# A fused three-layer block on one core: value projection spread over the heads, gate projection split, embedding projections moved

## The chip, the cores and the metric

The kernel runs on one core of a Trainium2 chip. The metric is the device time of one execution in microseconds (us), lower is better. The engines are TensorE (PE, with its weight loads PEld), VectorE (DVE), ScalarE (ACT), GpSimd (POOL) and SyncE (SP), which issues the DMAs of the weights. Each has its own stream of instructions, in order, and they meet through semaphores.

## The reference, cut to what matters

256 tokens of width 1024 pass through one block (adaptive modulation, sparse attention and convolution, feed-forward net, two layer norms) and then through two layers of another kind:

```
def second_block(x, p, ...):
    for i in range(2):
        hn = rms_norm(h, norm_mix[i])
        mix = gla_mixer(hn, ...) if i == 0 else diff_attn_mixer(hn, ...)
        h = h + mix
        h = h + swiglu_2(rms_norm(h, norm_ffn[i]), ffn_w_in[i], ffn_w_out[i])
        gate = jax.nn.sigmoid(rms_norm(h, ple_norm[i]) @ ple_w_gate[i])
        h = h + gate * (p[i] @ ple_w_proj[i])

def gla_mixer(h, w_in, w_gate_f, b_gate_f, w_gate_b, b_gate_b, g_out, w_out):
    q, k, v, r, zf, zb = split_cols(h @ w_in, [512, 512, 1024, 1024, 16, 16])
    la_f = heads(log_sigmoid(zf @ w_gate_f + b_gate_f) / 16, 128)
    ...
def diff_attn_mixer(h, ...):
    q, k, v = split_cols(h @ w_in, [1024, 1024, 1024])     # q, k: normed and rotated
    ... 8 heads: softmax of two score maps, a = p0 - lam * p1, o = a @ v ...
```

## The kernel before

Activations lie transposed, as 8 tiles of 128 channels by 256 tokens. Weights come in slabs of 512 output columns. A slab is loaded into one of two buffers `raw`, in ring order. ScalarE rounds it into `whi` and VectorE writes the rest `raw - whi` into `wlo` (function `low`), each in four quarters. The activations are split the same way (`ohi`, `olo`, for the differential layer `dhi`, `xlo`), and a product is three matmuls (`three`): high by high, low by high, high by low. Each projection is a phase of `plan()`; `gemm` on each engine walks its slabs and tiles, and the slab that follows is split during the one before it. The order on each engine is written out by hand.

The places that the change touches:

- `layer_norm` closes each sublayer of the first block. TensorE sums values and squares over channels. VectorE and ScalarE make mean, variance and scale (`rstd`), centre and scale `res`, and write `ohi`, `om`, `olo` tile by tile. TensorE fills the wait with `keep_warm`.
- The gated layer begins with `gla_z` (48 rows, in float32, from `om`), then `gla_q`, the sums of squares (`stats`), another `keep_warm`, the two gate products from `g_z`, and `gla_k`, `gla_v`, `gla_r`. The squares are added on POOL.
- Before its four heads ScalarE computes both halves of `silu(r)` and then the first `kd_tok`, which TensorE waits for.
- `ple(k)`: the projection `ple_proj{k}` (48 matmuls, copied by ScalarE into `pp`), then `stats`, then `ple_gate{k}`, two slabs, whose tiles VectorE scales (`gt`), ScalarE puts through the sigmoid (`sg`), POOL multiplies by `pp` (`prod`) and VectorE adds to `res`. After the first of them VectorE and ScalarE also make the operand `dhi`, `xlo` of `diff_q` from each tile.
- The differential layer: `diff_q`, `diff_k`, `diff_v`, then 8 heads: TensorE scores, VectorE maximum (`neg_max`), ScalarE exponential (`d_p`), VectorE weights, TensorE transposes, ScalarE copy (`d_pt`), TensorE product with `d_v`, VectorE copy (`d_o`). Then `out2`.

A phase whose first slab is in `WIDE` takes the channel tiles in the outer loop, so all four output tiles go on as soon as one operand tile is there. SP frees a `raw` buffer by a table: `reader_done = {"split": lo_ready, ..., "pe": z_done}`; `gla_z` is of kind `pe`.

## Time and profile before

| | us |
|---|---|
| median of 3 runs (range) | 1118.05 (1114.88 to 1119.05) |
| the profiled execution | 1114.69 |
| its span in the profile | 1112.5 |
| TensorE busy, share of the span | 1055.4, 95% |
| VectorE busy | 724.4, 65% |
| ScalarE busy | 555.6, 50% |

The span is what the trace covers of the profiled execution; 2.2 us lie outside it. TensorE's busy time is modelled from pipelined matmuls, so the rate is better read from the start of one to the start of the next. The granted clock of TensorE is given as a share of 2.4 GHz; its two levels are 1.00 and 0.50.

### The profile page before, as it was taken

Reading aid. Unit: us, or ns where it says so; the run is one execution under the profiler, and the core shown is the slowest. Engines: PE = TensorE matmul, PEld = TensorE weight load, DVE = VectorE, ACT = ScalarE, POOL = GpSimd, SP = SyncE. Lnnn points to the kernel's source line nnn. Section 1 sums busy time; section 2 is a strip of 40 time slices with the busy share of each in tenths; the row PEclk is TensorE's granted clock in tenths of the full one; section 3 lists DMA queues with packets and bytes.
Section 4 is the critical chain, followed back from the end, with each engine's and each line's share of the span. In section 5 each row is a group of like instructions: output and inputs, shape, how many; then the busy total and the mean of one; then the engine's idle time right before and its main releaser. Section 6 shows DMA issues by size and latency. Waiting matters only on the chain. (4 is left out here: it accounts for less than half of the span.)

```text
span 1112.5 us, 20252 instructions
## 1 busy us (share of the span) xinstructions
PE 1055.4 (95%) x7893; PEld 979.4 (88%) x7893; DVE 724.4 (65%) x1130; ACT 555.6 (50%) x958; POOL 225.1 (20%) x246
## 2 busy tenths in 40 slices
PE   6899998999999899999999999979987999999998
PEld 5577787999999698889999999978865999999997
DVE  5788758777655567767565656676768765655654
ACT  2224466545454676337545444656447754544453
POOL 0000013333312121022333311131110223332101
PEclk9989899999999999999999999989999999999999
DMA  9984452577557354404646455644440266554651
GB/s 352 401 308 158 143 199 76 175 262 263 150 156 221 99 216 149 155 1 163 216 155 222 115 158 183 228 151 152 152 152 1 94 210 205 172 163 139 191 189 39
DMA packets 183587, 192.78 MB, mean 173 GB/s; under 512 B 5913, under 2 KB 143426, under 8 KB 183522
## 3 DMA queue, kind: packets, MB, share of 16 engines
q1 hardware_dynamic: 182512, 191.15, 50.8%
q8 instruction: 43, 0.70, 0.3%
q0 software_dynamic: 144, 0.52, 0.2%
q10 hardware_dynamic: 866, 0.21, 0.1%
q14 instruction: 22, 0.18, 0.0%
HBM read 190.83 MB, written 1.05 MB: 172 GB/s over the span
## 5 line engine op out<-in xcount | busy, mean ns | idle before, releaser
L1395 DVE TENSOR_TENSOR wlo<-raw,whi 128x1024 fp32r<-128x1024 f32 (+2 forms) x316 | 360.8, 1187 | 69.8 <-ACT whi L892 69.3
L2089 PE MATMUL gemm<-ohi,whi 128*128 128x256 f32 x1376 | 387.4, 282 | 3.6 <-DVE olo L1435 1.7
L2090 PE MATMUL gemm<-olo,whi 128*128 128x256 f32 x1376 | 384.5, 279 | 0.0
L2091 PE MATMUL gemm<-ohi,wlo 128*128 128x256 f32 x1376 | 383.3, 279 | 0.0
L892 ACT ACTIVATE whi<-raw 128x1024 fp32r<-128x1024 f32 (+2 forms) x316 | 280.6, 954 | 62.1 <-PE gemm L2091 49.4
L2089 PEld LDWEIGHTS gemm<-ohi,whi 128*128 128x128 f32 x1376 | 258.5, 188 | 7.0 <-issue 4.5
L2090 PEld LDWEIGHTS gemm<-olo,whi 128*128 128x128 f32 x1376 | 258.7, 188 | 0.6 <-issue 0.5
L2091 PEld LDWEIGHTS gemm<-ohi,wlo 128*128 128x128 f32 x1376 | 258.6, 188 | 0.0
L2091 PE MATMUL gemm<-acthi,wlo 128*128 128x256 f32 x528 | 147.7, 280 | 0.0
L2089 PE MATMUL gemm<-acthi,whi 128*128 128x256 f32 x528 | 147.7, 280 | 0.0
L2090 PE MATMUL gemm<-actlo,whi 128*128 128x256 f32 x528 | 147.3, 279 | 0.0
L727 POOL TENSOR_TENSOR prod<-sg,ut 128x256 f32<-128x256 f32 x66 | 51.4, 780 | 263.1 <-DVE ut L1796 160.9
L2091 PEld LDWEIGHTS gemm<-acthi,wlo 128*128 128x128 f32 x528 | 99.2, 188 | 0.0
L2090 PEld LDWEIGHTS gemm<-actlo,whi 128*128 128x128 f32 x528 | 99.1, 188 | 0.0
L2089 PEld LDWEIGHTS gemm<-acthi,whi 128*128 128x128 f32 x528 | 98.9, 187 | 0.0
L1172 ACT ACTIVATE sg<-gt 128x256 f32<-128x256 f32 x66 | 27.6, 419 | 131.5 <-DVE gt L1796 91.4
L731 POOL TENSOR_TENSOR actlo<-prod,acthi 128x256 f32 (+1 forms) x63 | 70.3, 1116 | 0.0
L2090 PE MATMUL gemm<-xlo,whi 128*128 128x256 f32 x224 | 63.9, 285 | 0.0
L1796 DVE TENSOR_TENSOR ut<-gemm,rstd 128x256 f32<-128x256 f32 x44 | 18.4, 419 | 52.1 <-PE gemm L2091 52.1
L764 POOL TENSOR_TENSOR sq_sum<-sq_sum,dsq 128x256 f32<-128x256 f32 x28 | 24.1, 862 | 110.3 <-ACT dsq L911 99.1
L2321 PE MATMUL gemm<-om,raw 128*128 128x256 f32 x192 | 45.6, 395 | 0.0
L2089 PE MATMUL gemm<-dhi,whi 128*128 128x256 f32 x128 | 40.0, 313 | 5.6 <-DVE xlo L1432 4.4
(367 smaller groups left out, 1535.9 us busy)
## 6 DMA issues: line engine op xcount, KB each, us to landing
raw<-in_ffn_w_in SPq DMA_DIRECT2D x44, 1024.0 KB, 6.2
raw<-in_ffn_w_out SPq DMA_DIRECT2D x32, 704.0 KB, 5.8
part<-in_w_ada SPq DMA_DIRECT2D x32, 512.0 KB, 10.3
raw<-in_gla_w_in SPq DMA_DIRECT2D x6, 2048.0 KB, 7.8
raw<-in_diff_w_in SPq DMA_DIRECT2D x6, 2048.0 KB, 7.7
raw<-in_w_gate SPq DMA_DIRECT2D x11, 1024.0 KB, 6.3
raw<-in_w_up SPq DMA_DIRECT2D x11, 1024.0 KB, 8.5
raw<-in_w_down SPq DMA_DIRECT2D x16, 704.0 KB, 5.4
```

What stands on the lines that cost most here:

```text
L727: pool.tensor_tensor(tl(prod, j), tl(sg, j), tl(ut, j), ALU.mult).then_inc(prod_done, 1)
L731: pool.tensor_tensor(tl(actlo, t - 1), tl(prod, 1 - j), tl(acthi, t - 1).bitcast(F32), ALU.subtract).then_inc(actlo_ready, 1)
L764: pool.tensor_tensor(sq_sum[:, :], sq_sum[:, :], src, ALU.add).then_inc(squares_summed if last else sq_added, 1)
L892: act.activation(whi[hslot][:, q * w:(q + 1) * w], src[:, q * w:(q + 1) * w], ACT.Copy).then_inc(hi_ready, 1)
L1172: act.activation(tl(sg, j), tl(gt, j), ACT.Silu).then_inc(silu_done, 1)
L1395: dve.tensor_tensor(wlo[hslot][:, q * w:(q + 1) * w], src[:, q * w:(q + 1) * w], whi[hslot][:, q * w:(q + 1) * w].bitcast(F32), ALU.subtra ...
L1796: ins = dve.tensor_tensor(dst, bank[:, 0:T], rstd[:, 0:T], ALU.mult)
L2089: pe.matmul(dst, st_hi, mv_hi, start=start, stop=False)
L2090: pe.matmul(dst, st_hi, mv_lo, start=False, stop=False)
L2091: return pe.matmul(dst, st_lo, mv_hi, start=False, stop=stop_)
L2321: ins = pe.matmul(G[t][:, 0:T], w[:, k, t * P:(t + 1) * P], tl(om, k), start=k == 0, stop=k == KT - 1)
```

## The change

Four groups of edits.

- **Layer norms**: ScalarE squares the mean straight from the sums in PSUM, VectorE makes the variance before the mean, centres the first two tiles singly, and makes `om` of tile 0 itself.
- **Start of the gated layer**: the first embedding projection takes the place of `keep_warm`. `gla_q` comes first and is `WIDE`; the eight squares are added on VectorE; `gla_z` comes behind `stats` and is split in three like the others. ScalarE's second half of `silu(r)` comes behind the first `kd_tok`.
- **Embedding projections**: the phases `ple_proj1` and `ple_proj2` are gone. Their weights have buffers of their own, are split in `down0` and `ple_gate1`, and their matmuls (`projection_of`) stand in the layer norm and between `ple_gate1` and `diff_q`. `ple(k)` begins with `ple_gate{k}`, with `stats` behind its first tile.
- **Values**: `diff_v` is cut into 64 steps of three matmuls with 256 columns. 16 stand before the heads and six in each head. The scores wait for their own pair of rotated tiles only. The splits of the second value slab and of `out2`'s first slab move into the heads.

In the order ScalarE's and SP's edits, then VectorE's, then TensorE's:

```diff
-    ple = lambda k: [Phase(f"ple_proj{k}", 1, 2048, 8, 1), Phase(f"ple_gate{k}", 2, SLAB, 4, 1)]
+    ple = lambda k: [Phase(f"ple_gate{k}", 2, SLAB, 4, 1)]
...
-        WIDE = ("gate_up0", "out1", "out2")
+        WIDE = ("gate_up0", "gla_q", "out1", "out2")
...
+            def load_projection(n):
+                sp.wait_ge(tile_done, (PH["gate_up0"].tile0 + 4, PH["down1"].tile0 + KT)[n])
+                sp.dma_start(flat(pw[n], 2, D), kmaj(a["ple_w_proj_2"][n], 0, D)).then_inc(pw_in, 16)
...
-                me.next(mean_ready)
-                me.did(act.activation(sq_sum[:, :], mean[:, :], ACT.Square), mean_squared)
+                me.next(mean_done)
+                me.seen(mean_done)
+                me.did(act.activation(sq_sum[:, :], X[0][:, 0:T], ACT.Square, scale=1.0 / D), mean_squared)
...
-            gemm("gla_q")
+            for q in range(3):
+                ahead(PH["gla_q"], At(0), q)
             root(X[0], T + 2, 1.0 / D, 1, rstd[:, :])
+            ahead(PH["gla_q"], At(0), 3)
...
-                gemm(f"ple_proj{k}", evac(lambda at, t: tl(pp, t), pp_ready))
                 root(X[0], T, 1.0 / D, 1, rstd[:, 0:T])
...
+                    if k == 1 and m in (1, 2):
+                        projection_split(1, m - 1)
...
+            take_projection(0, 1, 2)
             log_exp()
             next_quarters("diff_q")
             root(X[0], T + 2, 1.0 / D, 1, rstd[:, :])
+            take_projection(3)
...
+                if i in (2, 5, 7):
+                    take_values({2: 1, 5: 2, 7: 3}[i])
+                if 3 <= i <= 6:
+                    ahead(*OUT2, i - 3)
                 if i == 6:
                     pair_root(0, X[1])
...
-                center(0)
-                center(2)
+                center(0, 1)
+                center(1, 1)
                 me.next(sd_ready)
...
                 scale(0, 1)
+                me.again(normed)
+                me.link(dve.tensor_scalar(tl(om, 0), tl(res, 0), g[:, 0:1], b[:, 0:1], ALU.mult, ALU.add))
                 scale(1, 1)
+                rest_alone(0)
+                center(2)
+                me.again(centered)
                 scale(2, 2)
-                rest(0)
                 center(4)
                 rest(1)
...
+            for n, copies in pp_copies(1):
+                dve.wait_ge(pp_done, n + 1)
+                for dst, bank in copies:
+                    ins = dve.tensor_copy(dst, bank)
+                ins.then_inc(pp_ready[0], 1)
+            dve.wait_ge(z_hi_ready, 1)
+            dve.tensor_tensor(z_lo[:, :], raw[PH["gla_z"].slot][:, 0:384], z_hi[:, :].bitcast(F32),
+                              ALU.subtract).then_inc(z_lo_ready, 1)
+            for t in range(1, KT):
+                dve.wait_ge(sq_ready, SQUARED + t + 1)
+                me.link(dve.tensor_tensor(sq_sum[:, :], tl(sq, 0) if t == 1 else sq_sum[:, :], tl(sq, t), ALU.add),
+                        gla_summed if t == KT - 1 else None)
-            for q in range(4):
+            for q in range(3):
                 low(PH["gla_k"], At(0), q)
             root()
...
+                    if k == 1 and m in (2, 3):
+                        projection_low(1, m - 2)
...
+                if i in (0, 1):
+                    low(*VALUES, 2 + i)
+                if 4 <= i <= 7:
+                    low(*OUT2, i - 4)
...
-                gemm(f"ple_proj{k}", pp_ready, shape="ple")
-                stats()
-                gemm(f"ple_gate{k}", ple_in, olo_from=start)
+                def after(at, t):
+                    if (at.i, t) == (0, 0):
+                        stats()
+                gemm(f"ple_gate{k}", ple_in, olo_from=next_operand(), after=after)
...
             layer_norm()
-            keep_warm(X[2], 4)
+            projection_of(0)
...
-            gemm("diff_v", v_ready, shape="token", operand=(dhi, xlo), after=lambda at, t: partners(6 + t) if at.i == 0 else None)
-            pe.wait_ge(qk_ready, 8)
-            pe.wait_ge(v_ready, 8)
+            value_steps(0, 8)
+            partners(6)
+            partners(7)
+            value_steps(8, 16)
...
             for i in range(NH + 2):
                 if i + 1 < NH:
                     scores(i + 1)
+                if i >= 2:
+                    h = i - 2
+                    banks.claim(X[2], mixed_ready)
+                    me.next(pt_ready)
+                    if h % 2 == 0:
+                        pe.wait_ge(v_ready, 4 + h // 2 + 1)
...
+                if i < NH:
+                    value_steps(16 + 6 * i, 22 + 6 * i)
+                if i in (6, 8):
+                    group_stats((i // 2 - 3,), ones[:, :], d_nsq, X[1:2])
                 if 1 <= i <= NH:
...
```

TensorE at the start of the gated layer, before: the end of the layer norm's sums (`res`, `ln_sq`), `keep_warm`, `gla_z` from `om`, and the first matmuls of `gla_q` (`gemm0` to `gemm3` and `aux0` to `aux3` are the eight PSUM banks).

```order
L2422 MATMUL aux0<-res_72,ones_56 128x256
L2424 MATMUL aux1<-ln_sq_114,ones_56 128x256
L2213 MATMUL aux2<-const_55,ones_56 128x512 x4
L2514 MATMUL aux1<-om_73,raw1_50 48x256 x8
L2089 MATMUL gemm0<-ohi_74,whi1_52 128x256
L2090 MATMUL gemm0<-olo_75,whi1_52 128x256
L2091 MATMUL gemm0<-ohi_74,wlo1_54 128x256
```

The same place now: the last of the 48 matmuls of the embedding projection (`pw_hi`, `pw_lo`) and the first of `gla_q`.

```order
L2201 MATMUL aux1<-p_hi_76,pw_hi0_119 128x256
L2202 MATMUL aux1<-p_lo_77,pw_hi0_119 128x256
L2203 MATMUL aux1<-p_hi_76,pw_lo0_121 128x256
L2201 MATMUL gemm0<-ohi_74,whi1_52 128x256
L2202 MATMUL gemm0<-olo_75,whi1_52 128x256
L2203 MATMUL gemm0<-ohi_74,wlo1_54 128x256
L2201 MATMUL gemm1<-ohi_74,whi1_52 128x256
L2202 MATMUL gemm1<-olo_75,whi1_52 128x256
L2203 MATMUL gemm1<-ohi_74,wlo1_54 128x256
```

`keep_warm` and `gla_z` have gone from between the sums and `gla_q`, and the channel tile is now the outer loop.

TensorE in the heads, before: the scores of one head (`d_k`, `d_q`), the transposes of the head before it (`d_p`) and the product of that head (`d_pt`, `d_v`).

```order
L2649 MATMUL gemm2<-d_k_163,d_q_162 128x256
L2649 MATMUL gemm3<-d_k_163,d_q_162 128x256
L2649 MATMUL gemm2<-d_k_163,d_q_162 128x256
L2649 MATMUL gemm3<-d_k_163,d_q_162 128x256
L2666 MATMUL aux0<-const_55,d_p_166 128x128 x4
L2676 MATMUL aux2<-d_pt_167,d_v_164 128x256 x2
```

Now: the end of a head's value steps, the transposes, the next head's scores and product, and the first of the 18 matmuls that follow.

```order
L2203 MATMUL aux1<-whi1_52,xlo_143 128x256
L2823 MATMUL aux0<-const_55,d_p_177 128x128 x4
L2792 MATMUL gemm0<-d_k_174,d_q_173 128x256
L2792 MATMUL gemm1<-d_k_174,d_q_173 128x256
L2792 MATMUL gemm0<-d_k_174,d_q_173 128x256
L2792 MATMUL gemm1<-d_k_174,d_q_173 128x256
L2809 MATMUL aux2<-d_pt_178,d_v_175 128x256 x2
L2201 MATMUL aux1<-whi1_52,dhi_142 128x256
L2202 MATMUL aux1<-wlo1_54,dhi_142 128x256
L2203 MATMUL aux1<-whi1_52,xlo_143 128x256
```

The 18 value matmuls of a head stand between the product and the transposes.

ScalarE in the last `ple`, now: the sum of squares (`dsq`), the root (`rstd`), the table of the sigmoid, and the split of `ple_gate2`'s second slab (`whi0`). Before, eight copies `pp` stood ahead of the root.

```order
L933 ACTIVATE dsq_138<-res_72 128x256
L962 ACTIVATE rstd_80<-aux0,eps_64 128x256
L963 ACTIVATE rstd_80<-rstd_80 128x256
L1320 ACT_TABLE_LOAD
L1320 ACTIVATE lam_63<-eps_64 128x1
L908 ACTIVATE whi0_51<-raw0_49 128x1024
L1333 ACTIVATE sg_148<-gt_147 128x256
L908 ACTIVATE whi0_51<-raw0_49 128x1024 x3
```

The split stands behind the root and its table, as before; what TensorE does meanwhile is no longer the projection.

## Rows read from the trace of the kernel before

**Rows 1.** Page, busy time of engines, and its groups by line.

```profile
PE 1055.4 (95%) x7893; PEld 979.4 (88%) x7893; DVE 724.4 (65%) x1130; ACT 555.6 (50%) x958; POOL 225.1 (20%) x246
...
L1395 DVE TENSOR_TENSOR wlo<-raw,whi 128x1024 fp32r<-128x1024 f32 (+2 forms) x316 | 360.8, 1187 | 69.8 <-ACT whi L892 69.3
```

**Rows 2.** Waits of TensorE: us in total, times, longest.

```profile
PE aux L2666 <- DVE d_p L2058: 7.3, 7, 1.7
...
PE gemm L2089 <- DVE xlo L1432: 4.4, 2, 3.5
...
PE aux L2602 <- ACT kd_tok L1259: 2.2, 1, 2.2
```

**Rows 3.** Stretches: PE, PEld, DVE, ACT, POOL busy, granted clock, DMA share, GB/s.

```profile
379.40:386.70 7.30, 6.14 (x16) 1.55 (x16) 5.05 (x11) 7.30 (x16) 0.00 (x0) 0.77 0.00 1
713.00:735.60 22.60, 22.60 (x192) 22.42 (x192) 17.38 (x23) 15.81 (x28) 10.17 (x10) 1.00 0.53 187
735.60:743.90 8.30, 2.71 (x20) 2.28 (x19) 6.40 (x11) 2.69 (x8) 3.22 (x4) 0.95 0.72 250
743.90:750.00 6.10, 6.10 (x29) 6.10 (x30) 2.84 (x3) 3.66 (x5) 0.73 (x1) 0.51 0.01 3
803.50:828.00 24.50, 24.23 (x100) 18.41 (x98) 15.50 (x14) 11.71 (x15) 3.88 (x2) 1.00 0.32 108
845.30:848.80 3.50, 2.56 (x16) 1.75 (x17) 3.40 (x11) 2.52 (x11) 0.00 (x0) 1.00 0.00 0
```

**Rows 4.** Timeline, layer norms and the gated layer's start: start, us, idle before.

```profile
184.29 0.35 PE L2089 MATMUL gemm<-ohi,whi 128*128 128x256 f32 x1 [1.75 <-DVE olo L1435]
...
374.15 3.60 PE L2213 MATMUL aux<-const,ones 128*128 128x512 f32 x8
379.39 0.60 PE L2514 MATMUL aux<-om,raw 128*48 128x256 f32 x2 [1.64 <-DVE olo L1435]
...
400.74 2.96 PE L2525 MATMUL aux<-g_z,wgate 16*128 16x256 f32 x16
...
391.35 0.71 ACT L1155 ACTIVATE sq<-res 128x256 f32<-128x256 f32 x2
```

**Rows 5.** Page, DMA issues: KB each, us from issue to landing.

```profile
raw<-in_gla_w_in SPq DMA_DIRECT2D x6, 2048.0 KB, 7.8
```

**Rows 6.** Timeline, the last ple.

```profile
1075.08 0.35 PE L2089 MATMUL gemm<-p_hi,whi 128*128 128x256 f32 x1 [0.61 <-DVE res L1682]
...
1082.15 0.36 PE L2089 MATMUL gemm<-ohi,whi 128*128 128x256 f32 x1 [0.55 <-DVE wlo L1395]
...
1082.89 1.28 ACT L1283 ACT_TABLE_LOAD   x1
...
1086.09 2.95 ACT L892 ACTIVATE whi<-raw 128x1024 fp32r<-128x1024 f32 x3
...
1089.15 2.89 DVE L1395 TENSOR_TENSOR wlo<-raw,whi 128x1024 fp32r<-128x1024 f32 x2
```

**Rows 7.** Timeline, end of the first ple and start of diff_q.

```profile
724.95 0.67 DVE L1432 SCALAR_TENSOR_TENSOR xlo<-res,cols_b,dhi 128x256 fp32r<-128x256 f32 x1 [0.89 <-ACT dhi L916]
...
743.99 0.48 DVE L1432 SCALAR_TENSOR_TENSOR xlo<-res,cols_b,dhi 128x256 fp32r<-128x256 f32 x1 [0.18 <-ACT dhi L916]
...
743.87 0.58 PE L2089 MATMUL gemm<-dhi,whi 128*128 128x256 f32 x1 [3.50 <-DVE xlo L1432]
```

**Rows 8.** Timeline, values and heads.

```profile
806.35 3.31 DVE L1395 TENSOR_TENSOR wlo<-raw,whi 128x1024 fp32r<-128x1024 f32 x2
...
841.90 1.28 DVE L2042 TENSOR_REDUCE neg_max<-gemm 128x2 f32<-128x512 f32 x2
...
845.41 0.68 DVE L2042 TENSOR_REDUCE neg_max<-gemm 128x2 f32<-128x512 f32 x1
...
855.84 0.63 PE L2666 MATMUL aux<-const,d_p 128*128 128x128 f32 x4 [1.16 <-DVE d_p L2058]
...
862.58 0.68 PE L2089 MATMUL gemm<-xhi,whi 128*128 128x256 f32 x1
```

More of the change, by code:

```diff
@@ L650, in _ @@
                       ("gate_up0", 0): parts(24, 25),
-                      **{("gate_up0", i): parts(23 + i) for i in range(3, 9)}, ("gla_z", 0): [load_gates]}
+                      **{("gate_up0", i): parts(23 + i) for i in range(3, 9)}, ("gate_up0", 9): [lambda: load_projection(0)],
+                      ("gla_z", 0): [load_gates], ("ple_gate1", 1): [lambda: load_projection(1)]}
             for ph in PHASES:
@@ L1186, in scaled_then_square @@
                     square0(at, t, 1)
+                    if at.it is None and at.i == 0:
+                        act.wait_ge(p_trans, 2)
+                        for half in range(2):
+                            projection_split(0, half)
                 gemm(f"down{k}", after=early if k else scaled_then_square)
@@ L1330, in _, with take_values @@
                 gemm(name, after=after)
-            gemm("diff_v", evac(v_dst(d_v), v_ready, v_scale))
+            VALUES, OUT2 = (PH["diff_v"], At(0)), (PH["diff_v"], At(1))
+            def take_values(j):
+                wait(act, tile_done, PH["diff_v"].tile0 + j + 1)
+                bank = VALUE_BANKS[j]
+                for tt in range(TT):
+                    ins = act.activation(d_v[:, tt * D + 256 * j:tt * D + 256 * (j + 1)], bank[:, tt * 256:(tt + 1) * 256],
+                                         ACT.Copy, scale=v_scale(tt))
+                me.did(ins, v_ready)
+            for q in range(4):
+                ahead(*VALUES, q)
+            take_values(0)
             def pair_root(g, bank):
@@ L1402, in body @@
                 def body(at):
+                    if ph.name == "down0" and at.it is None and at.i == KT - 1:
+                        for half in range(2):
+                            projection_low(0, half)
                     for t in range(ph.tiles):
@@ L1892, in _ @@
                 take_q(At(0), t, bank_of(PH["gla_q"], At(0), t)[0])
+            low(PH["gla_k"], At(0), 3)
             for b in range(4):
@@ L2159, in body @@
                             w = lambda v, k: v[:, k, t * P:(t + 1) * P]
-                        ks = {"down": range(FT), "ple": range(2)}.get(shape, order)
-                        layer = int(name[-1]) - 1 if shape == "ple" else 0
+                        ks = range(FT) if shape == "down" else order
                         for n_, k in enumerate(ks):
@@ L2170, in body @@
                             else:
-                                src = {"down": (acthi, actlo), "ple": (p_hi, p_lo)}.get(shape, operand)
-                                mv = [pick(b, k + 2 * layer) for b in src]
+                                mv = [pick(b, k) for b in ((acthi, actlo) if shape == "down" else operand)]
                                 ins = three(bank[:, 0:T], w(hi, k), w(lo, k), *mv, n_ == 0, n_ == len(ks) - 1)
@@ L2504, in _ @@
             layer_norm()
-            keep_warm(X[2], 4)
+            projection_of(0)
             start = next_operand()
-            ph = PH["gla_z"]
-            slot = ph.slot
-            pe.wait_ge(landed[slot], ph.landed[0])
+            gemm("gla_q", dve_read, olo_from=start)
+            stats(tok=True, summed=gla_summed)
+            pe.wait_ge(z_lo_ready, 1)
             banks.claim(X[1], z_ready)
             for k in range(KT):
-                pe.wait_ge(olo_ready, start + k + 1)
-                ins = pe.matmul(X[1][0:48, 0:T], raw[slot][:, 48 * k:48 * (k + 1)], tl(om, k),
-                                start=(k == 0), stop=(k == KT - 1))
+                ins = three(X[1][0:48, 0:T], z_hi[:, 48 * k:48 * (k + 1)], z_lo[:, 48 * k:48 * (k + 1)], tl(ohi, k),
+                            tl(olo, k), k == 0, k == KT - 1)
             ins.then_inc(z_done, 1)
-            gemm("gla_q", dve_read, after=lambda at, t: stats(tok=True) if t == 2 else None)
-            keep_warm(X[2], 2)
             pe.wait_ge(z_ready, 1)
```

176 lines of the change are left out of this document (121 added, 55 removed).

## The prediction

> **What bounds the kernel now.** I read the page first: TensorE is busy 95% of the span, every other engine far less [rows 1], so only what TensorE executes or waits for counts. Its steady rate is in the stretch 713.0 to 735.6: 192 matmuls in 22.6 us, 0.1177 us each with 256 columns [rows 3]. Then the waits of TensorE: the largest group is the transposes in the heads, seven waits for VectorE's `d_p`, 7.3 us; `diff_q` waits twice for `xlo`, up to 3.5 us; the first `kd_tok` costs 2.2 us [rows 2]. Third, the stretches: in the heads (845.3 to 848.8, one head) TensorE works 2.56 of 3.50 us, but VectorE 3.40, so VectorE sets the head's period; between `ple_gate1` and `diff_q` (735.6 to 743.9) TensorE works 2.71 of 8.30 us, and the 6.1 us behind it have a granted clock of 0.51, the lower of its two levels, 1.2 GHz [rows 3]. Last the timelines, for what is late at each place.
>
> **Work removed or added on TensorE.** The 96 projection matmuls are moved, not removed. `gla_z` changes from float32 to 24 split matmuls. The 192 value matmuls stay. So the gain can only be idle time that work fills, or a chain that gets shorter. I take each place in order of time.
>
> *First layer norm.* TensorE waits 1.75 us for the first `olo` and starts at 184.29 [rows 4]. The first tile's chain loses the hop through `mean` (one op, about 0.45 us) and half of the two centring ops (0.7 us), so the first `olo` is some 1.0 us earlier. But VectorE now does `center(2)`, `scale(2, 2)` and `center(4)` between `rest_alone(0)` and `rest(1)`, 0.68 us each: the second `olo` comes when it did, and TensorE needs it 1.4 us (12 matmuls) after the first. I take 0; bounds 0 and 1.2.
>
> *Start of the gated layer.* Before, `keep_warm` runs from 374.15, the first float32 matmul at 379.39 after 1.64 us of idleness, and the gates start at 400.74 and take 2.96 us [rows 4]: `gla_k` at 403.7. Now 48 projection matmuls run from 374.15 for 5.65 us, to 379.8; `gla_q`, 96 matmuls, follows without a wait, since `WIDE` needs a new `olo` only every 1.4 us and they come each 1.0 us: it ends at 391.1. `stats` needs the eighth square, which ScalarE ends at 391.35 + 0.71 = 392.06 [rows 4] as before, plus one add on VectorE: 392.5, a new wait of 1.4 us. With `stats` (0.9) and 24 matmuls (2.8) `gla_z` ends at 396.5. Behind `stats`, VectorE has three `low` of 1.19 us [rows 1] queued ahead of `g_z`, fed by ScalarE's splits from 392.1 at one per us: done about 396.4. Then `g_z` (0.85), so the gates run 397.4 to 400.4; the fourth `low` is done at 400.0. `gla_k` starts at 400.4: gain 3.2 us. What is late next: `reader_done` frees the buffer of `gla_z` at `z_done`, which was 386.7 and is now 396.5. The value slab behind it lands 7.8 us after its issue [rows 5], 404.3; its four splits, two ScalarE quarters at a time with VectorE behind, end near 409.7, and `gla_k` runs to 411.8. Hidden by 2 us. Bounds: 0, if that cover goes (landing 2 us later plus the new pauses), and 5.6, the whole projection.
>
> *First kd_tok.* Only one half of `silu(r)` stands ahead of it now and the table load is behind it. What is left of the wait is the copy itself, 0.6 us, and two hand-overs, about 0.8 us: gain 1.4 of 2.2 [rows 2]. Bounds 0 and 2.2.
>
> *The last ple.* The projection phase began at 1075.08, the gate at 1082.15 [rows 6]; the gate now begins at 1075.08, 7.07 us earlier. `stats` sits behind the first gate tile (0.45 us). The new wait: ScalarE's split of the second gate slab is queued behind `rstd` and the sigmoid's table load. Before, this ran under the projection. Load at 1082.89, three `whi` from 1086.09, last two `low` end at 1089.15 + 2.89 = 1092.04 [rows 6], 9.15 us behind the load's start, 8.8 without the pause for `gt` that ScalarE then had. Now the load can start at 1075.08 + 2.8 (tile) + 0.65 (`stats`) + 1.0 (root) = 1079.5, the slab is ready at 1088.3, and TensorE wants it at 1075.08 + 11.3 + 0.45 = 1086.85. It waits 1.4 us. Gain 7.07 - 0.45 - 1.4 = 5.2 us. Bounds 3.9 and 6.6.
>
> *The first ple and diff_q.* The same start, but here VectorE's chain (scale, `low`, `xlo`, add, for eight tiles) is the bound: the last `xlo` is at 743.99, 8 us after the gate's last matmul, and TensorE goes on at 743.87 [rows 7]. That chain starts with the table load, here as above 3.4 us earlier (1082.89 against 1079.5), and has the 0.4 us less: 3.8 us. Two more VectorE splits of 1.19 us go into it, but at tiles 2 and 3 where VectorE waits 0.89 us for `dhi` [rows 7]: net +0.5. So `diff_q` has its last two operand tiles 3.3 us earlier, at 740.5. TensorE ends the gate at 730.4 and the projection at 736.0, does six of the eight steps of the first tile and waits 2.4 us. The clock: before, the idle time of this place (5.6 of 8.3 us) was followed by 29 matmuls at 0.21 us instead of 0.1177, 2.7 us lost [rows 3]. With the projection in the pause only 2.4 us are idle at a stretch. I expect the full clock and 2.7 us. But ScalarE copies the projection (five copies, 2.8 us) ahead of its splits and root, so `block_sums` in the first slab of `diff_q` waits about 1.5 us for `d_sq`. Gain 3.3 + 2.7 - 1.1 = 4.9 us. Bounds 1.5 (clock falls again, longer ScalarE queue) and 8.
>
> The rule that bears on it is in the Trainium skill, TensorE: Matmul & The Clock Gate, section Part 1: The HAM clock gate: the half rate is the default, and only sustained activity keeps the full rate. By that rule the sum would be 2.7 us smaller here, and the removed `keep_warm` is a risk of its own.
>
> *Values and heads.* From the end of `diff_k` (803.4) to `out2` (862.58 [rows 8]) it takes 59.1 us, of which 24.5 are the values [rows 3]. Now only 16 of 64 steps come first. VectorE has two `low` beside POOL (806.35 + 3.31 [rows 8]), then two turns of 1.4 us with POOL's product between: 813.2. Then the heads begin. Head 0: maximum 1.5, exponential 1.9, then scores (1.0), six steps (18 x 0.1177 = 2.1) and transposes (0.5) on TensorE: 820.2. The period before is 845.41 - 841.90 = 3.51 us, all VectorE's [rows 8]. With one `low` it is 3.51 + 1.19 = 4.7 for six heads; TensorE has 2.56 + 2.1 = 4.66 at most, less some overlap. So both are nearly full at 4.6: six more heads end at 820.2 + 27.6 + 0.9 (group sums) = 848.7. Before, from the transposes of the seventh head (855.84 + 0.63) to `out2` took 6.1 us [rows 8]. Now ScalarE has `whi` and `pair_root` (2.2 us) queued ahead of the last exponential, and the last `take_values`: I estimate 7.0, `out2` at 855.7. Gain 6.9 us. Bounds: 0, if all added work lands on the heads' round trip (8 x 0.85 us), and 11, all waits gone.
>
> **Sum:** 0 + 3.2 + 1.4 + 4.9 + 6.9 + 5.2 = 21.6 us, so 1114.69 - 21.6 = 1093.1 for the profiled execution. The median of the runs is 3.4 us above that execution, and its lowest run is beside it. I place the forecast between: 1095.
>
> **Rivals.**
> *The heads run slower than their sums* (0.17). Each head is a loop over four engines, and ScalarE's order now has a split, a value copy or a root behind each `d_pt`. If the round trip sets 5.3 us, eight heads lose 5.6 us: gain 16, 1100.5. For it: VectorE and TensorE would both be near 100%. Against: one head's ScalarE work is 2.52 of 3.50 us [rows 3], with additions of 1 to 2 us below 4.7.
> *The clock falls in the new pauses* (0.12): behind the 2.4 us at `diff_q` and the pauses of 1.4 and 1.2 us around `gla_z`, 2.7 us each: gain 16, 1100. For it: at 379.4 to 386.7 the clock was 0.77 behind a pause of 1.64 us and sparse matmuls [rows 3, 4]. Against: in the heads it is 1.00 with 27% idle [rows 3].
> *Less waiting than worked out* (0.08): new waits at `stats` and the gate slab vanish, TensorE overlaps more in the heads: gain 27, 1089.5.
> *The change does not do what it says* (0.05): the gaps' chains get as much longer as work was put in, the value steps only move the wait. Gain below 5 us: 1112.
> *Slower* (0.03): the clock stays at its lower level through the heads. From 803.4 to 855.7 TensorE has 24.5 + 8 x 2.56 = 45 us of work at full clock; all at half clock costs 45 us more: 1140. It decides the sign from about 27 us of that work on. Against: the row of 1.00 in the heads, where TensorE now works more, not less.
>
> **Numbers.** My forecast, gain 17 to 26, has 0.55. A measurement of this kernel tells about 0.5%, 5.6 us, from no change. The first three rivals are also faster: 0.92 in all; 0.05 within 0.5%; 0.03 slower. The range that leaves out 2 in 10: from 1087 (third rival) to 1106, which takes in the first two rivals and half of both together.
>
> **What the profile after would show.** Right: `gla_k` 3 us earlier against the layer norm; a TensorE wait for `wlo` of 1 to 2 us between the two slabs of both `ple_gate`; the first `kd_tok` wait under 1 us; clock 1.00 in the first slab of `diff_q` with a wait for `xlo` of 2 to 3 us ahead; head period 4.6 us, transposes hardly waiting, a wait for ScalarE at the last head; VectorE above 95% there. Wrong: waits of TensorE for `raw` at `gla_v`, a head period above 5 us, or a clock of 0.5 at `gla_k`.

## The result and the profile after

The changed kernel takes 1100.48 us (median of 4 runs, 1096.44 to 1101.48), the kernel before in the runs beside it 1116.59 us (4 runs, 1114.88 to 1119.05). The ratio is 0.9851, 95% interval 0.9829 to 0.9873: 16.1 us faster. I forecast 1095, range 1087 to 1106. The profiled execution of the changed kernel took 1101.48 us with a span of 1099.7, which is 12.8 us below the span of before; my sum for that difference was 21.6.

The page, TensorE's row of the first part (to [rows 1]): it is busy for 1052.9 us instead of 1055.4, in a span that is 12.8 us shorter, so what went is nearly all idle time.

```profile
PE 1052.9 (96%) x7985; PEld 987.7 (90%) x7985; DVE 730.8 (66%) x1143; ACT 552.3 (50%) x946; POOL 221.2 (20%) x239
```

TensorE's waits in the changed kernel (what waits, for whom, us in total, times, longest), the rows that answer to [rows 2]:

```profile
PE gemm L2201 <- DVE wlo L1464: 4.1, 3, 1.5
PE gemm L2201 <- DVE xlo L1510: 2.6, 1, 2.6
PE aux L2809 <- ACT d_v L1388: 2.5, 2, 2.0
...
PE aux L2809 <- ACT d_pt L1425: 1.6, 2, 0.8
...
PE aux L2304 <- DVE sq_sum L1972: 1.4, 1, 1.4
PE gemm L2792 <- ACT d_p L1412: 1.3, 1, 1.3
...
PE aux L2647 <- DVE g_z L1979: 1.0, 1, 1.0
...
PE aux L2724 <- ACT kd_tok L1296: 0.7, 1, 0.7
```

The seven waits of the transposes for `d_p` (7.3 us) are gone. In their place stand 5.4 us of waits for ScalarE in the heads, and two new ones in front of the gates, 1.4 and 1.0 us. The first `kd_tok` wait fell from 2.2 to 0.7.

A further loss is no wait. Windows of the changed kernel around the gates (columns: busy time and instructions of each engine, granted clock, DMA share, GB/s):

```profile
398.00:400.00 2.00, 2.00 (x19) 2.00 (x18) 2.00 (x2) 1.97 (x4) 0.00 (x0) 1.00 0.00 0
400.00:402.00 2.00, 0.99 (x7) 0.67 (x6) 1.71 (x5) 0.33 (x1) 0.58 (x1) 1.00 0.27 24
402.00:404.00 2.00, 2.00 (x12) 1.74 (x11) 2.00 (x5) 0.00 (x0) 1.49 (x4) 0.74 0.90 315
404.00:406.00 2.00, 2.00 (x6) 1.15 (x6) 2.00 (x6) 0.00 (x0) 0.00 (x0) 0.50 1.05 407
406.00:408.00 2.00, 2.00 (x11) 2.00 (x11) 1.07 (x3) 0.00 (x0) 0.00 (x0) 0.50 1.05 409
408.00:410.00 2.00, 2.00 (x12) 2.00 (x11) 0.80 (x1) 1.89 (x2) 0.00 (x0) 0.56 1.05 410
```

The clock falls to its lower level (0.50, 1.2 GHz) in the gates and stays there for the first `gla_k` matmuls: 11 in 2 us instead of some 17. The profile of before has no such fall there. It has one 20 us sooner, at `gla_z` (0.77 in [rows 3]), and one in the heads; both stand in all three profiles of the kernel before that I have, and neither in this one. The heads of before:

```profile
835.20:838.60 3.40, 3.27 (x13) 2.10 (x14) 3.19 (x10) 2.23 (x9) 0.00 (x0) 0.50 0.00 0
```

The heads, from the timeline of the changed kernel (start, duration, instruction, in brackets the idle time before it and who ended it); the row 818.84 is the transposes of the first head:

```profile
818.84 0.60 PE L2823 MATMUL aux<-const,d_p 128*128 128x128 f32 x4
...
837.67 0.60 PE L2823 MATMUL aux<-const,d_p 128*128 128x128 f32 x4
839.77 1.10 PE L2809 MATMUL aux<-d_pt,d_v 128*128 128x256 f32 x4 [0.44 <-ACT d_v L1388]
843.72 0.60 PE L2823 MATMUL aux<-const,d_p 128*128 128x128 f32 x4
845.10 1.10 PE L2809 MATMUL aux<-d_pt,d_v 128*128 128x256 f32 x4 [0.78 <-ACT d_pt L1425]
848.20 0.60 PE L2823 MATMUL aux<-const,d_p 128*128 128x128 f32 x4
850.84 1.10 PE L2809 MATMUL aux<-d_pt,d_v 128*128 128x256 f32 x4 [2.05 <-ACT d_v L1388]
...
854.02 1.10 PE L2809 MATMUL aux<-d_pt,d_v 128*128 128x256 f32 x4 [0.78 <-ACT d_pt L1425]
```

Four periods from 818.84 to 837.67 are 4.71 us each. And two of these windows:

```profile
828.00:833.00 5.00, 5.00 (x39) 4.35 (x38) 3.69 (x9) 3.36 (x10) 0.00 (x0) 1.00 0.00 0
833.00:838.00 5.00, 5.00 (x39) 4.35 (x37) 4.89 (x13) 3.89 (x11) 0.00 (x0) 1.00 0.00 0
```

TensorE is never idle there, while VectorE is busy for 3.69 of 5 us in one of them. Over the four periods it is busy for 4.5 to 4.6 us in three and for 3.4 in the third. So TensorE has become the bound of the middle heads, with VectorE nearly full beside it. After the fifth head it waits for ScalarE.

To see where the 12.8 us came from I cut both spans at the same instructions of TensorE (start of a group to start of the next, us; worked out from the two timelines; `out0` counts from its second matmul, 0.2 us behind the first):

```
stretch                                        before   after    gain   forecast
start to out0                                  147.46  148.40    -0.9     0
out0 to gate_up0 (first layer norm)             36.83   37.12    -0.3     0
gate_up0                                       124.99  126.88    -1.9     0
down0                                           63.31   63.32     0       0
end of down0 to gla_k                           31.04   29.86    +1.2    +3.2
gla_k to the end of gla_r                       57.73   59.62    -1.9     0
end of gla_r to gate_up1                        56.80   55.36    +1.4    +1.4
gate_up1 and down1                             187.14  187.13     0       0
end of down1 to the end of diff_k               95.58   92.05    +3.5    +4.9
end of diff_k to out2                           61.70   56.27    +5.4    +6.9
out2 to the end of down2                       211.89  211.94     0       0
end of down2 to the end of the last gate        30.53   25.41    +5.1    +5.2
from there to the span's end                     7.50    6.34    +1.2     0
```

The profiles of the runs below tell which rows belong to the change. The last `ple` takes 30.5 us in all three profiles of the kernel before and 25.4 in all changed ones without the early split. From the end of `diff_k` to `out2` it is 61.5 to 61.7 against 56.3, or 58 where the clock falls in the last heads, in the changed ones with its order of the heads. The last row is 7.5 in all three and 6.3 in all eleven of changed kernels, with the same instructions in it; no run here explains that. The first row is no cost of the change: `out0` starts at 147.5, 148.3 and 150.1 in the three of before, and between 146.0 and 149.6 in the others. Of the 1.9 us from `gla_k` to the end of `gla_r`, the second profile of before has lost 1.5 too.

### The profile page after: what moved, and what is told of

It is laid out like the page before. It is cut to its first block, busy times and chain, and to the rows that moved or that the text cites. A ratio compares the mean times of both kernels' runs of the same rounds, so it can differ in the third digit from the quotient of the medians.

```text
span 1099.7 us, 20433 instructions
## 1 busy us (share of the span) xinstructions
PE 1052.9 (96%) x7985; PEld 987.7 (90%) x7985; DVE 730.8 (66%) x1143; ACT 552.3 (50%) x946; POOL 221.2 (20%) x239
## 4 chain that ended last, share of the span: by engine, by line
PE 54%; DVE 6%; ACT 4%; issue 1%; POOL 0%; DVEq 0%; ACTq 0%; POOLq 0%
PE gemm L2201 16%; PE gemm L2203 15%; PE gemm L2202 15%; DVE wlo L1464 2%; PE aux L2689 1%; ACT whi L908 1%; PE aux L2739 1%; PE aux L2809 1%; PE aux L2201 0%; PE gemm L2792 0%; PE aux L2203 0%; PE aux L2202 0%; PE aux L2745 0%; DVE state L2059 0%; DVE res L1937 0%
## 5 line engine op out<-in xcount | busy, mean ns | idle before, releaser
L1464 DVE TENSOR_TENSOR wlo<-raw,whi 128x1024 fp32r<-128x1024 f32 (+1 forms) x308 | 355.2, 1197 | 67.9 <-ACT whi L908 67.4
L908 ACT ACTIVATE whi<-raw 128x1024 fp32r<-128x1024 f32 (+1 forms) x308 | 276.4, 963 | 63.3 <-PE gemm L2203 43.1
L2201 PE MATMUL gemm<-acthi,whi 128*128 128x256 f32 x528 | 147.5, 279 | 0.0
L2430 PEld LDWEIGHTS gemm<-om,raw 128*128 128x128 f32 x192 | 38.7, 204 | 9.3 <-issue 3.6
```

Of the source, the lines that this page charges most:

```text
L908: act.activation(whi[hslot][:, q * w:(q + 1) * w], src[:, q * w:(q + 1) * w], ACT.Copy).then_inc(hi_ready, 1)
L1464: dve.tensor_tensor(wlo[hslot][:, q * w:(q + 1) * w], src[:, q * w:(q + 1) * w], whi[hslot][:, q * w:(q + 1) * w].bitcast(F32), ALU.subtra ...
L2201: pe.matmul(dst, st_hi, mv_hi, start=start, stop=False)
L2430: ins = pe.matmul(G[t][:, 0:T], w[:, k, t * P:(t + 1) * P], tl(om, k), start=k == 0, stop=k == KT - 1)
```

## The experiments

The name of each run stands behind its heading. The runs came in four batches; the kernel before ran beside each (medians 1115.85, 1115.90, 1115.67 and 1116.14 us). Times are compared with that of c_after.

**The changed kernel once more.** (c_after) No edit.

> The changed kernel itself once more, as the measure for the other runs on this chip. Expected: 1100.5 us, within 3 us. Its second profile tells whether three things seen in the first belong to the change or to that one execution: gate_up0 at 0.118 us a matmul where the kernel before had 0.117 (1.2 us over the phase), a start of out0 that is 0.95 us later, and the lower clock behind gla_z. Theory: the first two are of that execution (they go away or change sign), the clock at the gates and in the first gla_k matmuls is of the change (0.5 again). Rival: all three come back.

Measured: 1099.61 us (1098.68 to 1101.62), ratio 0.9852 (0.9832 to 0.9872). In its profile every stretch of the table is within 0.2 us of the first one's: `out0` starts at 148.52, `gate_up0` takes 126.88, from `gla_k` to the end of `gla_r` it is 59.7 with the same low clock. So the rival, that all three come back, was right for this pair. Later runs show that two of them are still no fixed cost: `out0` starts at 146.0 in e3_values, and `gate_up0` has the faster pace in e1_warm and others (last section).

**Dummies around the gates, and at diff_q.** (e1_warm)

```
+            keep_warm(X[2], 1)                               # 512 columns
+            keep_warm(X[2], 1, const[:, NC - 256:NC])        # 256 columns
             stats(tok=True, summed=gla_summed)
...
+            keep_warm(X[2], 1)
             pe.wait_ge(z_ready, 1)
...
+  if first and ph.name == "diff_q" and (t, n_) == (0, 6):
+      keep_warm(X[2], 3, tl(res, 0, 2))
```

> The changed kernel with dummy matmuls on constants in three pauses of TensorE: 512 and 256 columns ahead of the statistics behind gla_q, 512 columns ahead of the wait for g_z, three times 512 columns ahead of the seventh operand tile of diff_q. Theory (the pauses of 1.40, 1.00 and 2.62 us let the clock fall to its lower level): the gates take 2.96 us again and not 3.81, from the first gla_k matmul to the end of gla_r it is 57.6 us and not 59.5, the 31 matmuls behind the wait at diff_q run at 0.118 us and not at 0.21 (2.1 us): together 5 us less than the changed kernel, 1095.5. Rival A (the clock fell for another cause, such as the thin matmuls of gla_z and of the gates): the clock is still 0.5 at the gates or the first gla_k matmuls, and at most 2 us come back. Rival B (the dummies end later than what they wait for): the clock is 1.00, but stats, gates or diff_q start 0.5 to 1 us later, 1098.

Measured: 1101.71 us, ratio 0.9872 (0.9851 to 0.9893), 2 us above c_after (the intervals overlap) instead of 5 below. Windows around the gates:

```profile
400.00:402.00 2.00, 1.85 (x12) 1.57 (x12) 1.97 (x6) 0.00 (x0) 1.63 (x3) 1.00 0.68 166
402.00:404.00 2.00, 2.00 (x12) 1.55 (x9) 2.00 (x5) 0.00 (x0) 0.44 (x2) 0.83 1.04 408
404.00:406.00 2.00, 2.00 (x11) 2.00 (x11) 1.97 (x6) 0.00 (x0) 0.00 (x0) 0.50 1.05 410
```

TensorE had no pause of over 0.2 us since 394, and the clock fell all the same at 403.3: rival A. At `diff_q` the run says nothing on the clock, because I chose a bank that ScalarE was still to read; the dummies themselves waited and then held up the matmuls behind them, and the stretch from `down1` to the end of `diff_k` is 3.1 us longer than in c_after:

```profile
741.64 4.32 PE L2324 MATMUL aux<-res,ones 128*128 128x512 f32 x6 [3.44 <-ACT pp_run L1357]
```

**The second gate slab's first splits ahead of the root, in both ples.** (e2_split)

```
 def ple(k):            # ScalarE; VectorE has next_lows in the same place
+    next_quarters(f"ple_gate{k}")
     root(X[0], T, 1.0 / D, 1, rstd[:, 0:T])
```

> The changed kernel with the first two quarters of the second ple_gate slab split ahead of the root, in both ples, where ScalarE is idle for 2.5 us and VectorE for 3.3 us. Theory (the wait of 1.5 us between the two slabs is ScalarE's split queued behind the sigmoid's table load, and VectorE's chain to diff_q starts with these splits): the wait between the slabs goes in both ples, 1.5 and 1.4 us, and the last xlo of diff_q comes 1 to 2.4 us earlier: 3.9 to 5.3 us less than the changed kernel, about 1096. Rival (the slab has not landed by then, or VectorE's splits hold up the first gate tile and all behind it): the waits move to rstd or gt and the time stays within 1 us of the changed kernel.

Measured: 1095.76 us (1093.33 to 1096.54), ratio 0.9812 (0.9794 to 0.983): 3.9 us less, as the theory said. Its waits of TensorE, to be held against 4.1 in three waits for `wlo` above:

```profile
PE gemm L2203 <- DVE xlo L1511: 2.3, 1, 2.3
...
PE gemm L2203 <- DVE wlo L1465: 1.2, 1, 1.2
```

The two between the slabs are gone (what is left is the one at `gla_v`), the last stretch of the table takes 23.66 us instead of 25.41, and from `down1` to the block sums of `diff_q` it is 44.8 instead of 48.3. Of these 3.5 us, 1.5 are the slab's wait; the clock, 0.62 in the 4.5 us behind the wait for `xlo` in the changed kernel, was 1.00 here behind a pause that is only 0.3 us shorter.

**The first layer norm in the order of before.** (e4_ln) `center` and `scale` two tiles at a time, the first `om` on ScalarE again, the square from `mean`; for the first norm alone.

> The changed kernel with the first layer norm's order of before (the second one keeps the new order). My forecast had the new order at 0. Theory: 0.5 to 1 us slower than the changed kernel: the wait for the first olo is 1.75 us again and not 0.56, the one between the first and the second operand tile (0.66 us) goes. Rival (the new order itself cost the 2 us that gate_up0 took longer in the profile after): 1 to 3 us faster, with gate_up0 back at 123.5 us.

Measured: 1103.70 us (1101.75 to 1104.36), ratio 0.9893 (0.9875 to 0.991): 4.1 us slower, more than either theory. The profile of its fastest run has the expected wait of 1.7 us for the first `olo`, and starts `gate_up0` 36.88 us behind `out0`, 0.35 sooner than c_after (37.23). The reason is the clock in the norm's sums, first c_after, then this kernel:

```profile
178.21 1.19 PE L2525 MATMUL aux<-mean,ones 128*128 128x256 f32 x2 [2.40 <-POOL sq_sum L831]
```

```profile
177.57 0.67 PE L2546 MATMUL aux<-mean,ones 128*128 128x256 f32 x2 [2.42 <-POOL sq_sum L831]
```

The same two matmuls behind the same pause take 1.19 us at the lower clock and 0.67 at the full one. The other runs of this kernel were longer at a lower mean clock (spans 1101.4 to 1102.6 at 0.981 to 0.983, c_after 1096.9 to 1099.8 at 0.986 to 0.989), so the 4.1 us go with the clock: the span times its mean clock is 1083 us here and 1084 in c_after. The profile shows one of the places, the last heads, where the clock fell at 849.3 and the stretch to `out2` took 57.9 us instead of 56.3. Why all five runs had the lower clock isn't shown, and the 4.1 us can't be read as the worth of the new order. The rival is out: `gate_up0` is only 0.7 us shorter, by the pause ahead of the second operand tile, and its pace is that of c_after.

**The value matmuls ahead of the heads again.** (e3_values)

```
-            value_steps(8, 16)
+            value_steps(8, 64)
...
-                if i < NH:
-                    value_steps(16 + 6 * i, 22 + 6 * i)
```

> The changed kernel with all 192 value matmuls ahead of the first scores again and all four value copies there; the rest of the heads as in the changed kernel. Theory (the steps fill waits of the heads): the block sums of diff_k to out2 take 59 us instead of 53.7, and seven waits of the transposes or products for VectorE or ScalarE, some 7 us in all, are back: 5.4 us slower than the changed kernel, 1105. Rival (the value steps only move the waits): within 1 us of the changed kernel.

Measured: 1108.93 us (1105.32 to 1112.08), ratio 0.9935 (0.9911 to 0.9959): 9.3 us slower, where I had said 5.4. From the end of `diff_k` to `out2` it is 66.7 us, 5.0 more than in the kernel before. The edit leaves the rest of the change in the heads in place: the product ahead of the transposes, a single bank for the products, and the splits of `out2`'s slab. First TensorE's wait for VectorE's copy out of that bank, then a window over one head:

```profile
PE aux L2808 <- DVE d_o L2158: 5.1, 4, 2.1
```

```profile
847.91:852.56 4.65, 3.57 (x19) 2.17 (x19) 4.54 (x12) 3.71 (x11) 0.00 (x0) 1.00 0.01 2
```

Three heads in a row take 4.64 us instead of the 3.51 of before, with VectorE busy for 4.54 of them; the 1.1 us more is one `low` in each. So the value steps do fill waits, as the theory has it; but a large part of what they fill is time that the change itself adds, VectorE's splits of `out2` in four heads. The copy comes late because VectorE is full; whether a second bank would help isn't shown. The clock was also at its lower level for longer in these heads than in the profile of before. The 9.3 us are the worth of the steps in this order, not of the change against before, which is 5.4.

**Dummies at the first layer norm, and at diff_q in a free bank.** (e5_warm)

```
+            keep_warm(X[2], 2)
+            keep_warm(X[2], 1, const[:, NC - 256:NC])
             first_sums()
...
+                                keep_warm(G[3], 3, tl(res, 0, 2))
```

> The changed kernel with dummy float32 matmuls in two pauses of TensorE: 1280 columns in the 2.40 us ahead of the first layer norm's sums (behind which the clock was 0.50 from 178 to 181 us in four of the five profiles of changed kernels, not in the fifth), and 1536 columns in the 2.6 us ahead of the seventh operand tile of diff_q, in a bank that is free there. In the run with dummies behind gla_q the clock fell all the same at 403 us, while TensorE had been busy without a pause of over 0.2 us since 394. Theory now (a fall needs more than one pause, it depends on the moment): with these two pauses full the clock stays at 1.00 in both places, the first gate_up0 matmul comes 1 to 1.5 us earlier and 2.1 us come back at diff_q: up to 3 us less than the changed kernel, 1097. Rival (dummies don't hold the clock): 0.5 again at 178 or 744, and the time stays or is up to 1 us longer.

Measured: 1097.18 us (1095.91 to 1099.24), ratio 0.9833 (0.9812 to 0.9855): 2.4 us less. The runs overlap a little with those of c_after (1095.9 to 1099.2 against 1098.7 to 1101.6), so it is the profile that carries the reading. The norm's sums in this profile:

```profile
176.43 0.67 PE L2527 MATMUL aux<-mean,ones 128*128 128x256 f32 x2 [0.27 <-POOL sq_sum L831]
...
178.23 3.60 PE L2324 MATMUL aux<-const,ones 128*128 128x512 f32 x8
182.41 0.36 PE L2201 MATMUL gemm<-ohi,whi 128*128 128x256 f32 x1 [0.58 <-DVE olo L1513]
```

`out0` to `gate_up0` takes 35.69 us instead of 37.23, and `down1` to the block sums 46.87 instead of 48.28, with a clock of 1.00 in both places. The theory holds for these two pauses. (The expectation counts four falls in five profiles; over all runs the fall at the first norm came in all eight profiles with the new order and no dummies, and in none of the three with the old order.)

**The gates behind the first tile of gla_k.** (e6_gates) `gemm("gla_k", dve_read, after=gates)`, with the 16 gate matmuls in `gates` for tile 0.

> The changed kernel with the 16 gate matmuls moved behind the first tile of gla_k, so that 24 full matmuls stand between gla_z and them. Theory (what stands ahead of the fall at 403 us is one run of thin work, gla_z and the gates, and the wait for g_z): the wait of 1.0 us for g_z goes or shrinks to the wait for the fourth wlo of gla_k (0.5 us), and the clock stays at 1.00 from 400 to 411: gla_z to the end of gla_r takes 3 to 3.5 us less than in the changed kernel, 1097. Rival A (the wait goes, the clock falls all the same): 0.5 to 1 us less. Rival B (the later gates hold up the first head of the gated layer): what is won at gla_k is lost ahead of out1.

Measured: 1105.30 us (1099.43 to 1107.11), ratio 0.9884 (0.986 to 0.9908): 5.7 us slower, as neither theory said. TensorE and VectorE:

```profile
404.36 0.39 PE L2201 MATMUL gemm<-ohi,whi 128*128 128x256 f32 x1 [3.59 <-DVE wlo L1464]
```

```profile
400.88 0.84 DVE L1979 TENSOR_TENSOR g_z<-aux,rstd 16x256 f32<-16x256 f32 x2 [0.25 <-PE aux L2203]
401.75 1.42 DVE L1988 SCALAR_TENSOR_TENSOR g_q<-gemm,rstd 128x256 f32<-128x256 f32 x4
403.09 1.21 DVE L1464 TENSOR_TENSOR wlo<-raw,whi 128x1024 fp32r<-128x1024 f32 x1
```

`gla_k` needs its fourth `wlo`, and VectorE makes that behind `g_z` and four evictions. I had put the wait at 0.5 us; it is 3.6. In the changed kernel the gates cover it. The profile accounts for 2.7 of the 5.7 us between `down0` and the end of `gla_r`; the rest goes with more falls of the clock elsewhere, 1.7 us of it in the heads (mean 0.979 in that execution, 0.983 to 0.989 in the others).

**Another order in the heads.** (e7_heads)

```
-                    value_steps(16 + 6 * i, 22 + 6 * i)
+                    value_steps(*VALUE_CUTS[i:i + 2])
+            VALUE_CUTS = (16, 25, 32, 39, 46, 52, 58, 64, 64)
```

and on ScalarE, for i = 6: the last split ahead of `d_pt`, then the last exponential, `take_values(3)`, and only then the first group's root; on TensorE the second group's sums behind the last transposes.

> The changed kernel with another order in the heads: the 48 value steps go 9, 7, 7, 7, 6, 6, 6, 0 to the eight heads instead of 6 each, the last value copy and the last exponential stand ahead of the first group's root on ScalarE, and the second group's sums behind the last transposes on TensorE. Theory (what is left of TensorE's waits in the heads, 1.4 + 0.4 + 0.8 + 2.1 + 0.8 us, is ScalarE's queue and a last set of value steps that ends after the last scores): scores to out2 takes 43.2 us instead of 46.4, and the waits for d_v go: 1096.5. Rival (VectorE, nearly full, sets the period): the heads with seven steps take as much longer as the end gets shorter, within 1 us of the changed kernel.

Measured: 1095.94 us (1093.42 to 1100.32), ratio 0.982 (0.9793 to 0.9848): 3.7 us less. The profile gives 2.2 of them to the heads (first scores to `out2` 44.1 us instead of 46.4, I had said 43.2): the seven-step heads last 5.1 us instead of 4.7, and the end is shorter. Another 1.1 us are at the gates, which ran at the full clock in this execution. The edit moves value steps, ScalarE's order and the second group's sums at once; what each is worth isn't shown. What is left of the waits:

```profile
847.41 1.10 PE L2819 MATMUL aux<-d_pt,d_v 128*128 128x256 f32 x4 [1.45 <-ACT d_pt L1430]
```

**gla_z on 128 stationary columns** (e8_wide_z) instead of 48; the other 80 hold values that nothing reads.

> The changed kernel with gla_z on 128 stationary columns instead of 48 (the 80 others hold values that nothing reads), so that these 24 matmuls fill the array's columns; their number and moving columns are as before. Theory (TensorE was busy when the clock fell at 403 us behind dummies, and in the kernel before it fell behind gla_z too, so gla_z's narrow matmuls bring it about): the clock stays at 1.00 through the gates and gla_k, 2.96 us for the gates and 57.7 us to the end of gla_r: 2.5 to 3 us less than the changed kernel, 1097. Rival (the pauses ahead of it, or the moment alone): 0.5 again behind 402 us and the time of the changed kernel.

Measured: 1098.50 us (1095.93 to 1099.00), ratio 0.9839 (0.9815 to 0.9862), which is no difference from c_after. The clock fell:

```profile
402.00:404.00 2.00, 2.00 (x8) 1.40 (x8) 2.00 (x6) 0.00 (x0) 0.08 (x1) 0.63 1.05 404
404.00:406.00 2.00, 2.00 (x11) 2.00 (x11) 1.55 (x4) 0.00 (x0) 0.00 (x0) 0.52 1.05 410
```

The theory is out. The low stretch is shorter than in the changed kernel, but so it is in e7_heads, where nothing was touched here.

**Four edits together.** (e9_best) The early split, the dummies at the first norm, two dummies at `diff_q` and the heads' new order.

> The changed kernel with the early split of the ple_gate slabs, the dummies ahead of the first layer norm's sums, two dummies (1024 columns) in the pause at diff_q, and the new order in the heads. If the four add up: 3.9 + 1.5 + 1 + 3.2 us less than the changed kernel, 1090. Rival (they share a pause, or the clock falls elsewhere instead): 1093 to 1095.

Measured: 1089.11 us (1087.17 to 1089.62), ratio 0.9754 (0.9736 to 0.9773): 10.5 us less than c_after and some 27 less than before; I had said 1090. The edits add up, and this version beats both kernels. Its waits of TensorE:

```profile
PE aux L2825 <- ACT d_pt L1431: 2.2, 2, 1.5
...
PE aux L2317 <- DVE sq_sum L1983: 1.4, 1, 1.4
PE gemm L2212 <- DVE wlo L1474: 1.2, 1, 1.2
```

**The kernel before once more.** (c_before) No edit.

> The kernel before once more, for a second profile. In seven of nine profiles of changed kernels without dummies there the clock was 0.50 for some 3.5 us behind the pause of 2.4 us ahead of the first layer norm's sums, and in all of them behind 402 us (for 3.4 or 6.8 us), while the one profile of before had neither. Theory (the fall at the first layer norm depends on the moment, the one at the gates belongs to the change): 1116 us, this profile may have the fall near 177 us, and has none between 398 and 415 us. Rival (both depend on the moment): a fall at the gates here too.

Measured: 1116.92 us (1113.78 to 1119.06), ratio 1.0002 (0.9986 to 1.0018). Its profile has a fall behind the gates too, a little later:

```profile
404.00:406.00 2.00, 2.00 (x14) 1.78 (x14) 1.33 (x4) 1.79 (x2) 0.00 (x0) 1.00 1.04 407
406.00:408.00 2.00, 2.00 (x13) 1.67 (x12) 2.00 (x7) 1.53 (x2) 0.00 (x0) 0.76 1.01 389
408.00:410.00 2.00, 2.00 (x11) 2.00 (x11) 2.00 (x2) 1.97 (x3) 0.00 (x0) 0.50 0.08 25
```

So that fall doesn't belong to the change alone (the rival); the one at the first norm was not there.

**The kernel before with the dummies at the first norm.** (e10_before_warm) The same lines as in e5_warm.

> The kernel before with dummy float32 matmuls (1280 columns) in the 2.4 us ahead of the first layer norm's sums. Theory (the fall there strikes the kernel before in some executions too): 0.5 to 1.5 us less than before, 1115, and no run near its highest. Rival (the fall there came with the change): within 0.3 us of before.

Measured: 1115.78 us (1114.16 to 1117.80), ratio 0.9998 (0.9985 to 1.001). No gain: `out0` to `gate_up0` takes 36.87 us with them and 36.83 without. The rival.

## Why the forecast was right, and what of it was not

The sign and the range were right, and 1100.5 lies 5.5 us above the forecast. That is where I had put the first two rivals (1100.5 and 1100), and the gain of 16 us lies just below the 17 to 26 that I gave my forecast. Of the signs of being wrong one came true, a clock of 0.5 at `gla_k`; of the signs of being right two failed, `gla_k` 3 us earlier (1.2) and the full clock in the first slab of `diff_q`. The mechanism of each part was found in the profile, but the sum was too large, and the time lies in the range because that took in the first two rivals. The parts:

- *The last ple*, forecast 5.2, measured 5.1, with the wait of 1.4 us for the second slab. That e2_split takes this wait away confirms its cause: ScalarE's splits stood behind the root and the table load.
- *First kd_tok*, 1.4 forecast; 1.4 us in its stretch and a wait of 0.7.
- *Values and heads*, 6.9 forecast, 5.4 measured. The period was 4.71 us in the middle heads against 4.6. I had VectorE set it at 4.7 and TensorE just below; it is TensorE that is never idle there, and VectorE has 1.3 us to spare in one of the four. What I missed is a wait of 0.4 us in the sixth head, where the product waits for a value copy that ScalarE makes late (the head takes 6.05 us, 0.9 of it the group sums that I had counted), and 0.1 us in each period. The six heads behind the first took 29.4 us, my term for them was 28.5. e7_heads got 2.2 us back with another order of the end, which fits ScalarE's queue as its cause but doesn't single it out.
- *The first ple and diff_q*, 4.9 forecast, 3.5 measured. The wait for `xlo` is 2.6 us (2.4 forecast), and the one for `d_sq` 0.2 (1.5 forecast). The term that failed is the clock, where I counted 2.7 us for the full rate. It fell again behind the pause of 2.6 us, for a shorter time. e5_warm, with that pause full, has the full clock and 1.4 us.
- *Start of the gated layer*, 3.2 forecast, 1.2 measured. The gates started 2.5 us nearer to `down0` than before, 0.9 less than worked out. The rest went in the gates, which took 4.2 us instead of 2.96 at the lower clock. In e1_warm, e5_warm, e7_heads, e8_wide_z and e9_best, where the clock fell only behind them, the gain is 2.1 to 2.5 us. This is the rival of the clock in the new pauses, at the place that I named, but with the wrong cause: it falls without the pauses (e1_warm), and once in the kernel before. Another 1.9 us were lost behind it in `gla_k`, where my sum had none. Nor did the sum count the fall at `gla_z` that went away.
- *First layer norm*, forecast 0, bounds 0 and 1.2. With the clock held (e5_warm) the new order is worth 1.1 us against before, 35.69 against 36.83; without, the sums run at half the clock and it is -0.3. The second operand tile comes late, as I said, by 0.4 to 0.6 us.
- *gate_up0* took 1.9 us more. 0.6 are that second tile. The rest is a slower pace at a full granted clock, which came and went between executions (last section).

What the sum left out altogether is that the clock's falls move from execution to execution. The span times its mean granted clock, a measure that leaves most of this out, is some 1096 us for before (median of its runs) and 1084 for c_after: 12 us less, and still well short of my 21.6. So the sum was too large in its terms too, above all at the gates, at `diff_q` and in the heads. One reading was also too kind: against the rival of the clock I held that it is 1.00 in the heads. That row covers one head of before; ten us sooner, in the window of before that stands with the result, it is 0.50.

One thing stays open. The fall at the first norm came in 8 of 8 profiles with the new order and in 0 of 3 with the old, behind a pause of 2.4 us in all eleven. But it begins between 0.4 us ahead of the end of that pause and its end, ahead of the first instruction that the two orders have differently. I can't say whether this is chance. What brings about the fall at the gates is open too: neither the pauses nor the narrow matmuls of `gla_z` by themselves.

## What to carry to other kernels

When work moves from one engine's busy stage into another stage's waits, price the queue behind every engine of that stage: here the wait between the gate slabs and those for `d_v` and `d_pt` came from a root, a split or a copy that stood one place too early on ScalarE, and putting two quarters of a split ahead of a table load, in two places, was worth 3.9 us, part of it clock. Look which engine is never idle in the windows before naming the bound, and look at the granted clock over the whole stage, not in one head of it. A dummy matmul pays only in a pause that is really followed by the lower clock, in a bank that nobody has still to read; elsewhere it brought nothing or cost time. And an edit of 1% needs its profile beside a second one of the same kernel, since the runs of one kernel differ by 0.6% here, part of it clock. When an edit takes work back out of a stage, see what else of the change still stands in it: in e3_values it was VectorE's splits, and the run overstates what the value steps gave.

## What the runs showed that I had not expected

The runs of one kernel differ by their granted clock, but not by that alone: the kernel before had a span of 1110.2 us at 0.988 and of 1117.4 at 0.979, and at 0.984 its spans reach from 1111.4 to 1117.6. The Trainium skill says of the same gate (TensorE: Matmul & The Clock Gate, section Part 1: The HAM clock gate) that the number of slow matmuls of one kernel varies from run to run, which these runs bear out in the middle of a kernel: the 30 matmuls behind the pause at `diff_q` took 6.5 us in the first profile of the kernel before and 5.4 in the second, behind the same pause of 3.5 us.

The clock fell at 403 us while TensorE had been busy for 9 us with no pause over 0.2 us (e1_warm), and held at `diff_q` in e2_split behind a pause of 2.3 us.

At a granted clock of 1.00 the 96 matmuls of one `gate_up0` slab took 11.20 us in some profiles (before, c_before, e1_warm and e5_warm to e10_before_warm) and 11.31 in others (after, c_after, e2_split, e3_values, e4_ln), slab after slab, except that in e6_gates and e7_heads the first slabs went at 11.31 and the others at 11.20; in `gate_up1` it was 11.31 in every profile. That is 1.1 us over `gate_up0`. It follows neither the code nor the clock that the profile shows, and no run here explains it.
